# TensorE's products of zeros at the layer changes and in the first attention heads left out

## The chip, the cores and the metric

The kernel runs on one core of one Trainium2 chip. The metric is the device time of one execution in microseconds. Before the change it is 1459.41 us, the median of three runs from 1458.01 to 1461.78.

## What is computed

Two blocks of a network for 256 tokens of width 1024, batch 1, float32. The first block is one layer: four mixers beside each other (latent attention, pooling, a state-space mixer and a gated recurrence), merged by gates, a feed-forward part and a gate with a side input `p`. The second is two layers: a mixer (dilated attention in the first, stick-breaking attention in the second), and a mixture of experts with 16 experts, each followed by a layer norm.

```python
x = x + merged @ w_out[l]
h2 = rmsnorm(x, g_mlp[l])
x = x + jnp.square(jax.nn.relu(h2 @ w_ff1[l])) @ w_ff2[l]
...
for layer in range(DEPTH_2):
    ...
        mixed = mixer_dilated(x, dil_w_in[occ], dil_w_out[occ], rel_table)
    ...
        mixed = mixer_stick_breaking(x, sb_w_in[occ], sb_w_out[occ])
    ...
    x = layer_norm(DEEPNORM_ALPHA * x + mixed, ln1_g[layer], ln1_b[layer])
    ffn = moe_ffn(x, router_w, router_b, exp_w_gate[layer], exp_w_up[layer], exp_w_down[layer])
    x = layer_norm(DEEPNORM_ALPHA * x + ffn, ln2_g[layer], ln2_b[layer])
```

## The kernel before

Each engine has its own instruction list, and the lists meet at semaphores. The weights stream once: SyncE's queue loads them in halves into a ring of six places (`w_ring`), ScalarE writes the high part of each as fp16 into `w_hi` (L1356), VectorE the low part into the ring's place (L1729), and TensorE makes three products for each tile: high by high, high by low, low by high. The dense products are those of `gemm_tok` (L687), `split_T` (L967, L969), the feed-forward output (L992), the products of `p` (L1016), and those of the experts (L1145, L1194). When TensorE is through with a half, it signals `w_used`, and the place is loaded anew.

Between two parts of the network the 256 tokens, in two tiles of 128, are normalized: VectorE adds the result from PSUM and makes sums (L2115, L2304), GpSimd takes the reciprocal root (L591), VectorE scales into `x_norm` (L1723, L1776). `act_transposes` (L657 to L670) then turns each tile on TensorE, 8 transposes of 128x128 for each (L668), and ScalarE and VectorE copy them as high and low parts (L1356, L1734) or as float32 (L1355, L1722). The next dense products wait for that. The document numbers these places by the argument of `act_transposes`: change 1 is ahead of `w_out`, 2 ahead of the feed-forward part, 3 ahead of the gate with `p`, 4 ahead of the dilated attention's projections, 5 and 7 ahead of the experts, 6 ahead of the stick-breaking projections. In changes 5 and 7 the router's 32 products (L1139, float32, 16 columns each) come first.

`idle_turns(n, bank)` (L652 to L655) issues n products of a zero tile, 128x128 by 128x512 in bfloat16, into a PSUM bank that nobody reads before it is written again. They are issued behind the last real product and ahead of the wait for the first normalized tile (`before` of `act_transposes`: 12), behind the transposes (4, in change 6 eight), ahead of the products of `p` (L1008: 12) and in change 1 (L951 and L954: 10 and 4).

The attentions run in stages over 8 pairs of heads, with an order written out by `staged`. In the dilated attention (L1113 to L1121) each step has the late scores (`dil_late`, L1048), turns of older probabilities (L1075), the early scores (`dil_early`, L1061) and the products with the values (L1106, L1109); VectorE adds a bias from GpSimd (L623) and takes maxima (L2231, L2235), ScalarE the exponentials (L1584). Zeros stand in its first two steps: 8 ahead of the late scores and 6 behind them. In the stick-breaking attention (L1323 to L1327) a step has `sb_pv` (L1319), `sb_scores` (L1295, L1296) and `sb_r` (L1305, L1307); VectorE clips (L2522, L2527) and ScalarE takes exponentials and logarithms (L1703, L1711, L1693), with a table load for each switch between them. Zeros stand in its steps 1 to 3: 8, 12 and 8.

Of the kernel before, what the change touches and what calls it, by code (L numbers as in the profile page):

```python
# [27 lines left out]
P = 128  # L28
# [144 lines left out]
def build(nc, a, out):  # L173

    ctx = ExitStack()
    with ctx:
        sems = {}

        def sig(name):
            if name not in sems:  # L180
                sems[name] = ctx.enter_context(nc.semaphore(name))
            return sems[name]

        def sb(name, shape, dt=F32):
            return ctx.enter_context(nc.sbuf_tensor(name, shape, dt))
# [17 lines left out]
        ps = ctx.enter_context(nc.psum_tensor("ps", [P, 8, 512], F32))  # L203
# [82 lines left out]
        zero16 = sb("zero16", [P, 512], BF16)  # L286
# [102 lines left out]
        def staged(i, *stages):  # L389

            for stage, behind in stages:
                if 0 <= i - behind < H2 // 2:
                    stage(i - behind)
# [244 lines left out]
        def _(pe):  # L638
# [10 lines left out]
                        ins = pe.transpose(ps[:, first_bank + k // 2, o:o + P], src[:, t, k * P:(k + 1) * P], ident)  # L649
                    ins.then_inc(sig(sem_name), 1)  # L650

            def idle_turns(n, bank):  # L652

                for _ in range(n):
                    pe.matmul(ps[:, bank, :], zero16[:, 0:P], zero16[:, :], start=True, stop=True)  # L655

            def act_transposes(i, before=None):  # L657

                if i:
                    pe.wait_ge(sig("xp_act"), 4 * i)  # L660
                    pe.wait_ge(sig("xp_dve"), 4 * i)
                if before is not None:
                    idle_turns(12, before)
                for t in range(T):
                    pe.wait_ge(sig(f"xn{t}_ready"), i + 1)
                    for k in range(KD):
                        o = (k % 2) * 256 + t * P
                        ins = pe.transpose(ps[:, 4 + k // 2, o:o + P], x_norm[:, t, k * P:(k + 1) * P], ident)  # L668
                        if t == T - 1:
                            ins.then_inc(sig("xp_pe"), 1)  # L670
# [69 lines left out]
            for c in range(KM):  # L740
                o = (c % 2) * S
                pe.matmul(ps[:, 4 + c // 2, o:o + S], up[:, 0, c * P:(c + 1) * P], band[:, c, 0:S],
                          start=True, stop=False, skip_group_check=True)
                ins = pe.matmul(ps[:, 4 + c // 2, o + P:o + S], up[:, 1, c * P:(c + 1) * P], band[:, c, S:384],
                                start=False, stop=True, skip_group_check=True)
# [6 lines left out]
            for b, k0, kn in ((0, 0, 2), (1, 2, 1)):  # L752
                w_h, w_l = weights(10 + b)
                for t in range(T):
                    hi, lo = slice(t * P, (t + 1) * P), slice(S + t * P, S + (t + 1) * P)
                    for h in range(2):
                        c = slice(h * 384, (h + 1) * 384)
                        for k in range(kn):
                            for i, (u, v) in enumerate(((hi, w_h), (hi, w_l), (lo, w_h))):
                                ins = pe.matmul(ps[:, 4 + 2 * t + h, 0:384], cT[:, k0 + k, u], v[:, k, c],  # L760
                                                start=(k0 + k + i == 0), stop=(k0 + k == 2 and i == 2),
# [14 lines left out]
            for b in range(2):  # L776
                w_h, w_l = weights(14 + b)
                for t in range(T):
                    hi, lo = slice(t * P, (t + 1) * P), slice(S + t * P, S + (t + 1) * P)
                    for h in range(2):  # L780
                        c = slice(h * 512, (h + 1) * 512)
                        for i, (u, v) in enumerate(((hi, w_h), (hi, w_l), (lo, w_h))):
                            ins = pe.matmul(ps[:, 4 + 2 * t + h, :], cT[:, 3 + b, u], v[:, 0, c],
                                            start=(b + i == 0), stop=(b == 1 and i == 2), skip_group_check=True)
# [163 lines left out]
                branch(i, yT, 1, 1)  # L948

            pe.wait_ge(sig("branch"), 3)  # L950
            idle_turns(10, 0)  # L951
            pe.wait_ge(sig("branch"), 4)
            act_transposes(1)
            idle_turns(4, 0)  # L954
            gemm_tok(22, 0, 512, 1)
            gemm_tok(23, 2, 512, None, True)

# [12 lines left out]
                                            stop=(kk == KD - 1), skip_group_check=True)  # L970
                    ins.then_inc(sig("w_used"), 1)

            act_transposes(2, 4)
            idle_turns(4, 0)
            for i in range(8):
                if i >= 2:
                    pe.wait_ge(sig("ff1_out"), i - 1)
# [4 lines left out]
            for i in range(8):  # L982
                pe.wait_ge(sig("hid_lo"), i + 1)
                for b in range(2):
                    w_h, w_l = weights(2 * (FF0 + 8 + i) + b)
                    for t in range(T):
                        for k in range(2):
                            kk = KM * i + 2 * b + k
                            c = slice(t * P, (t + 1) * P)
                            for u, v in ((hid_hi, w_h), (hid_hi, w_l), (hid_lo, w_h)):  # L990
                                for h in range(2):
                                    ins = pe.matmul(ps[:, 2 * t + h, :], u[:, kk, c], v[:, k, h * 512:(h + 1) * 512],  # L992
                                                    start=(kk == 0 and u is hid_hi and v is w_h),
                                                    stop=(kk == 31 and u is hid_lo), skip_group_check=True)
# [10 lines left out]

            pe.wait_ge(sig("pT"), 1)
            pe.wait_ge(sig("rel_row"), 1)
            idle_turns(12, 4)  # L1008
            pe.wait_ge(sig("x_res"), 2)
            for b in range(2):  # L1010
                w_h, w_l = weights(80 + b)
                for t in range(T):
                    hi, lo = slice(t * P, (t + 1) * P), slice(S + t * P, S + (t + 1) * P)
                    for i, (u, v) in enumerate(((hi, w_h), (hi, w_l), (lo, w_h))):
                        for h in range(2):
                            ins = pe.matmul(ps[:, 2 * t + h, :], pT[:, b, u], v[:, 0, h * 512:(h + 1) * 512],  # L1016
                                            start=(b + i == 0), stop=(b == 1 and i == 2), skip_group_check=True)
# [5 lines left out]
            def qkv(n0, g, base, aT, ready):  # L1023

                for s in range(6):
                    pe.wait_ge(sig("qkv_out"), base + 1 + s + g * 6)
                    if s < 4:
                        split_T(n0 + s, aT, (s % 2) * 4, ready, g * 12)
                    else:
                        gemm_tok(n0 + s, (s % 2) * 4, 512, None, False, aT, g * 12)  # L1030

            pe.wait_ge(sig("ple_gate"), 3)
            act_transposes(4)
            idle_turns(4, 0)
            with pe.Fori(0, 3) as g:
                qkv(DIL0, g, 0, act16, lambda b: act_ready(4, b))
            pe.wait_ge(sig("qkv_out"), 20)
# [73 lines left out]
                ins.then_inc(sig("dil_pv"), 1)  # L1111

            for i in range(KD + 2):  # L1113
                if i < 2:
                    idle_turns(8, 7)
                staged(i, (dil_late, 0))
                if i < 2:
                    idle_turns(6, 7)
                staged(i, (lambda m: dil_turn(m, 5), 2), (lambda m: dil_turn(m, 0), 1), (dil_early, 0),
                       (lambda m: dil_turn(m, 1), 1), (lambda m: dil_turn(m, 2), 1), (dil_spread, 1), (dil_pv, 2),  # L1120
                       (lambda m: dil_turn(m, 3), 1), (lambda m: dil_turn(m, 4), 1))  # L1121
# [7 lines left out]

            def experts(layer, n0, turn):  # L1130

                act_transposes(turn, 4)
                idle_turns(4, 0)
                pe.wait_ge(sig("xp_act"), 4 * turn + 4)
                pe.wait_ge(sig("xp_dve"), 4 * turn + 4)
                pe.wait_ge(sig("ld_router"), 16)
                for t in range(T):
                    for k in range(KD):
                        ins = pe.matmul(ps[:, 0, t * NE:(t + 1) * NE], actT[:, k, t * P:(t + 1) * P], router_w[:, k, :],  # L1139
                                        start=(k == 0), stop=(k == KD - 1))  # L1140
# [140 lines left out]

            experts(0, MOE0, 5)

            act_transposes(6, 4)
            idle_turns(8, 0)
            qkv(SBI0, 0, 18, sbq16, lambda b: pe.wait_ge(sig("aT_lo"), 3 + b))
            pe.wait_ge(sig("qkv_out"), 26)

# [33 lines left out]

            sb_scores(0)  # L1323
            for i in range(H2 // 2 + 6):
                if 1 <= i < 4:
                    idle_turns((8, 12, 8)[i - 1], 7)
                staged(i, (sb_pv, 6), (sb_scores, -1), (sb_r, 3))  # L1327

            def sb_o_ready(_, b):
# [1252 lines left out]
```

## Time and profile before

| what | value |
|---|---|
| median of three runs | 1459.41 us |
| the profiled execution | 1456.31 us, span 1454.5 us |
| TensorE matmul busy | 1375.5 us, 95% of the span, 7578 products |
| TensorE weight loads busy | 754.6 us, 52% |
| VectorE busy | 923.7 us, 64% |
| ScalarE busy | 698.4 us, 48% |
| GpSimd busy | 93.2 us, 6% |
| mean granted TensorE clock | 0.984 |

The span is the time from the first to the last instruction of the profiled execution; 1.8 us of its time lie around it. Matmuls are pipelined and overlap in the record, so a busy TensorE is not one at its peak. The granted clock is 1.0 at 2.4 GHz and 0.5 at 1.2 GHz. An engine's idle time costs something only where it is on the chain that ends last.

### The profile page before, as it was taken

How to read it: one execution, taken by the hardware profiler on the slowest of the kernel's cores; microseconds unless marked ns; L12 is line 12 of the kernel's file. 1: busy time of each engine (PE TensorE's matmuls, PEld its weight loads, DVE VectorE, ACT ScalarE, POOL GpSimd, SP SyncE). 2: the span in 40 equal slices, each digit the busy share in tenths (PEclk: the TensorE clock that was granted, in tenths of full speed). 3: DMA queues.
4: the chain of work that ended last, by engine and by line, in shares of the span. 5: the costliest groups of instructions: out<-in, count | busy, mean ns of one | idle time of the engine just before them, and what ended most of it. 6: DMA issues, size and time to landing. Idle time of an engine off the chain costs nothing.

```text
span 1454.5 us, 18623 instructions
## 1 busy us (share of the span) xinstructions
PE 1375.5 (95%) x7578; PEld 754.6 (52%) x7578; DVE 923.7 (64%) x1106; ACT 698.4 (48%) x682; POOL 93.2 (6%) x56
## 2 busy tenths in 40 slices
PE   6999997799999889999999999999989999999996
PEld 4685554345644436555567545444445545454442
DVE  6586755767864575555576575575666757665574
ACT  5476765235543344444456335454534653454451
POOL 0000000000000021000042021000004000300000
PEclk9999999899999989999999999999999999999999
DMA  9475433455656635666610446676837222666682
GB/s 316 131 242 174 145 127 126 147 173 172 218 189 207 233 125 180 204 201 202 202 52 2 145 146 211 223 260 212 309 117 231 86 87 96 214 212 222 212 269 78
DMA packets 152649, 258.03 MB, mean 177 GB/s; under 512 B 8881, under 2 KB 81532, under 8 KB 152572
## 3 DMA queue, kind: packets, MB, share of 16 engines
q1 hardware_dynamic: 152572, 256.96, 53.7%
q8 instruction: 54, 0.88, 0.2%
q14 instruction: 23, 0.19, 0.0%
HBM read 255.87 MB, written 1.07 MB: 177 GB/s over the span
## 4 chain that ended last, share of the span: by engine, by line
PE 86%; DVE 6%; ACT 3%; issue 3%; DVEq 1%; DMA 1%; POOL 1%; SPq 0%; POOLq 0%; ACTq 0%
PE ps L1145 17%; PE ps L687 17%; PE ps L967 11%; PE ps L1194 11%; PE ps L969 6%; PE ps L992 5%; PE ps L702 3%; PE ps L921 2%; DVE w_ring L1729 1%; PE ps L655 1%; ACT w_hi L1356 1%; PE ps L1075 1%; PE ps L1223 1%; PE ps L1182 1%; PE ps L1106 1%
## 5 line engine op out<-in xcount | busy, mean ns | idle before, releaser
L1729 DVE SCALAR_TENSOR_TENSOR w_ring<-w_ring,w_hi 128x2048 f16<-128x2048 f32 (+2 forms) x206 | 465.0, 2270 | 203.2 <-ACT w_hi L1356 202.0
L1356 ACT ACTIVATE w_hi<-w_ring 128x2048 f16<-128x2048 f32 (+2 forms) x206 | 381.9, 1865 | 250.1 <-PE ps L687 69.8
L687 PE MATMUL ps<-w_hi,actT 128*128 128x512 f16 (+2 forms) x832 | 247.5, 377 | 5.7 <-DVE actT L1734 5.7
L967 PE MATMUL ps<-actT,w_hi 128*128 128x512 f16 x640 | 208.6, 379 | 1.5 <-issue 1.2
L969 PE MATMUL ps<-actT,w_ring 128*128 128x256 f16 x640 | 174.6, 273 | 0.0
L687 PE MATMUL ps<-w_ring,actT 128*128 128x512 f16 (+2 forms) x416 | 156.9, 377 | 0.0
L1145 PE MATMUL ps<-w_ring,arena 128*128 128x512 f16 x384 | 146.3, 381 | 0.0
L1356 ACT ACTIVATE arena<-ps 128x512 f16<-128x512 f32 (+6 forms) x87 | 60.6, 709 | 172.2 <-PE ps L969 78.7
L1145 PE MATMUL ps<-w_hi,arena 128*128 128x512 f16 x448 | 138.4, 379 | 0.0
L687 PEld LDWEIGHTS ps<-w_hi,actT 128*128 128x128 f16 x832 | 82.2, 99 | 100.7 <-issue 6.5
L1194 PE MATMUL ps<-w_hi,arena 128*128 128x512 f16 x384 | 102.5, 379 | 2.8 <-DVE arena L2459 2.8
L967 PEld LDWEIGHTS ps<-actT,w_hi 128*128 128x128 f16 x640 | 62.7, 98 | 78.3 <-issue 3.2
L1145 PE MATMUL ps<-arena 128*128 128x512 f16 x320 | 100.3, 383 | 0.0
L1729 DVE SCALAR_TENSOR_TENSOR w_ring<-w_ring,arena 128x2048 f16<-128x2048 f32 x32 | 72.6, 2290 | 23.6 <-ACT arena L1356 23.6
L1194 PE MATMUL ps<-w_ring,arena 128*128 128x512 f16 x256 | 76.1, 379 | 0.0
L1145 PEld LDWEIGHTS ps<-w_hi,arena 128*128 128x128 f16 x448 | 44.1, 99 | 50.3
L969 PEld LDWEIGHTS ps<-actT,w_ring 128*128 128x128 f16 x640 | 62.7, 98 | 7.6
L992 PE MATMUL ps<-w_hi,arena 128*128 128x512 f16 x256 | 66.0, 379 | 0.0
L687 PEld LDWEIGHTS ps<-w_ring,actT 128*128 128x128 f16 x416 | 41.0, 99 | 45.8 <-issue 1.1
L591 POOL TENSOR_TENSOR stats<-stats 128x1 f32<-128x1 f32 x14 | 9.6, 688 | 842.1 <-DVE stats L2326 509.5
L1194 PEld LDWEIGHTS ps<-w_hi,arena 128*128 128x128 f16 x384 | 37.4, 98 | 48.3 <-DVE arena L2459 3.6
L1637 ACT ACTIVATE arena<-ps 128x512 f32<-128x512 f32 x16 | 9.6, 597 | 109.6 <-PE ps L1145 109.6
(411 smaller groups left out, 1840.4 us busy)
## 6 DMA issues: line engine op xcount, KB each, us to landing
w_ring<-in_dil_w_in SPq DMA_DIRECT2D x36, 1024.0 KB, 5.1
w_ring<-in_w_ff SPq DMA_DIRECT2D x32, 1024.0 KB, 5.2
w_ring<-in_exp_w_gate SPq DMA_DIRECT2D x64, 512.0 KB, 4.0
w_ring<-in_exp_w_up SPq DMA_DIRECT2D x64, 512.0 KB, 5.1
w_ring<-in_exp_w_down SPq DMA_DIRECT2D x32, 1024.0 KB, 5.0
w_ring<-in_w_in SPq DMA_DIRECT2D x24, 1024.0 KB, 5.2
w_ring<-in_sb_w_in SPq DMA_DIRECT2D x12, 1024.0 KB, 5.6
w_ring<-in_w_branch SPq DMA_DIRECT2D x8, 1024.0 KB, 5.0
```

Of the source, the lines that this page charges most:

```text
L655: pe.matmul(ps[:, bank, :], zero16[:, 0:P], zero16[:, :], start=True, stop=True)
L687: ins = pe.matmul(ps[:, bank + t, 0:cols], aT[:, kk, u], v[:, k, :], start=(kk + i == 0), stop=(kk == KD - 1 and i == 2), skip_group_check ...
L702: ins = pe.matmul(ps[:, bank + c // 2, o:o + S], v[:, k, cols], act16[:, kk, u:u + S], start=(kk + i + c % 2 == 0), stop=(kk == KD - 1 and ...
L921: ins = pe.matmul(ps[:, 4 * (i % 2) + 2 * t + h, :], yT[:, kk, u], v[:, k, h * 512:(h + 1) * 512], start=(kk + j == 0), stop=(kk == KM - 1 ...
L967: pe.matmul(ps[:, bank + c, :], w_h[:, k, cols], aT[:, kk, :], start=(kk == 0), stop=False, skip_group_check=True)
L969: ins = pe.matmul(ps[:, bank + c, 0:S], w_l[:, k, cols], aT[:, kk, 0:S], start=False, stop=(kk == KD - 1), skip_group_check=True)
L992: ins = pe.matmul(ps[:, 2 * t + h, :], u[:, kk, c], v[:, k, h * 512:(h + 1) * 512], start=(kk == 0 and u is hid_hi and v is w_h), stop=(kk ...
L1075: ins = pe.transpose(ps[:, 5 + i % 2, k * P:(k + 1) * P], e[:, k * P:(k + 1) * P], ident)
L1145: ins = pe.matmul(ps[:, bank, :], u[:, kk, c], v[:, k, :], start=(kk + m == 0), stop=(kk == KD - 1 and m == 2))
L1194: ins = pe.matmul(ps[:, 2 * t + h, :], u[:, b, c], v[:, f, h * 512:(h + 1) * 512], start=False, stop=(last and f == 1 and u is hT_lo), ski ...
L1356: return act.activation(dst, src, ACT.Copy, scale=scale)
L1729: dve.scalar_tensor_tensor(out=lo16(h)[:, 0:kn * c], in0=w_ring[:, h % RING, 0:kn * c], scalar=W_POW, in1=hi16(h)[:, 0:kn * c], op0=ALU.mu ...
```

## The change

It takes out `idle_turns`, all its calls and the argument `before` of `act_transposes`: 154 products in one execution. All waits stay, in their order. The four products of zeros that open the accumulation of the experts (L1276) stay too.

```diff
-            def idle_turns(n, bank):
-
-                for _ in range(n):
-                    pe.matmul(ps[:, bank, :], zero16[:, 0:P], zero16[:, :], start=True, stop=True)
-
-            def act_transposes(i, before=None):
+            def act_transposes(i):
 
                 if i:
                     pe.wait_ge(sig("xp_act"), 4 * i)
                     pe.wait_ge(sig("xp_dve"), 4 * i)
-                if before is not None:
-                    idle_turns(12, before)
                 for t in range(T):
...
             pe.wait_ge(sig("branch"), 3)
-            idle_turns(10, 0)
             pe.wait_ge(sig("branch"), 4)
             act_transposes(1)
-            idle_turns(4, 0)
             gemm_tok(22, 0, 512, 1)
...
-            act_transposes(2, 4)
-            idle_turns(4, 0)
+            act_transposes(2)
...
             pe.wait_ge(sig("rel_row"), 1)
-            idle_turns(12, 4)
             pe.wait_ge(sig("x_res"), 2)
...
             act_transposes(4)
-            idle_turns(4, 0)
...
             for i in range(KD + 2):
-                if i < 2:
-                    idle_turns(8, 7)
                 staged(i, (dil_late, 0))
-                if i < 2:
-                    idle_turns(6, 7)
...
-                act_transposes(turn, 4)
-                idle_turns(4, 0)
+                act_transposes(turn)
...
-            act_transposes(6, 4)
-            idle_turns(8, 0)
+            act_transposes(6)
...
             for i in range(H2 // 2 + 6):
-                if 1 <= i < 4:
-                    idle_turns((8, 12, 8)[i - 1], 7)
                 staged(i, (sb_pv, 6), (sb_scores, -1), (sb_r, 3))
```

## Rows read from the trace of the kernel before

**Rows 1.** Page: granted clock in 40 slices, in tenths; ending chain by engine.

```profile
PEclk9999999899999989999999999999999999999999
...
PE 86%; DVE 6%; ACT 3%; issue 3%; DVEq 1%; DMA 1%; POOL 1%; SPq 0%; POOLq 0%; ACTq 0%
```

**Rows 2.** Products of zeros, line L655: ns shortest/median/longest, first and last start.

```profile
L655 PE MATMUL ps<-zero x154: 378/379/634, 292.6 to 1206.5; 128*128 128x512 bf16 x154
```

**Rows 3.** Windows of busy us per engine; PEclk is the granted clock.

```profile
core 0: us, PE busy (x) PEld busy (x) DVE busy (x) ACT busy (x) POOL busy (x), PEclk, DMA share, GB/s
225.70:229.00 3.30, 3.30 (x13) 1.92 (x13) 3.13 (x8) 3.27 (x6) 0.00 (x0) 0.50 0.00 0
508.90:512.30 3.40, 3.40 (x9) 1.19 (x10) 2.64 (x5) 3.40 (x4) 0.00 (x0) 0.50 0.31 114
536.30:543.00 6.70, 4.36 (x15) 2.51 (x16) 5.89 (x13) 3.95 (x9) 5.10 (x3) 0.50 0.00 1
821.20:833.20 12.00, 10.43 (x72) 7.41 (x70) 8.89 (x13) 4.95 (x8) 0.81 (x2) 1.00 0.27 88
1068.80:1072.10 3.30, 3.30 (x12) 1.86 (x11) 1.90 (x4) 2.82 (x5) 0.00 (x0) 0.50 0.00 0
1212.10:1215.50 3.40, 3.40 (x10) 1.19 (x9) 3.40 (x3) 0.79 (x1) 0.00 (x0) 0.50 0.00 0
```

**Rows 4.** Timeline, change 4: start, us, engine, line, tiles, count, idle before.

```profile
538.33 1.97 PE L668 MATMUL ps<-mats,x_norm 128*128 128x128 f32 x8 [2.90 <-DVE x_norm L1723]
540.09 1.91 PE L655 MATMUL ps<-zero 128*128 128x512 bf16 x4
542.31 0.60 PE L967 MATMUL ps<-actT,w_hi 128*128 128x512 f16 x1 [0.31 <-DVE actT L1734]
```

**Rows 5.** Line L829, weight loads: 60 to 220 us; then 225 to 229.

```profile
L829 PEld LDWEIGHTS ps<-arena x10: 192/192/192, 145.8 to 207.1; 128*128 128x128 f32 x10
...
L829 PEld LDWEIGHTS ps<-arena x2: 333/333/333, 226.2 to 226.5; 128*128 128x128 f32 x2
```

**Rows 6.** Timeline, layer change 1: the zeros.

```profile
292.61 2.32 PE L655 MATMUL ps<-zero 128*128 128x512 bf16 x10
```

**Rows 7.** Timeline, layer change 2.

```profile
320.23 2.75 PE L655 MATMUL ps<-zero 128*128 128x512 bf16 x12
...
327.78 0.38 PE L967 MATMUL ps<-actT,w_hi 128*128 128x512 f16 x1 [1.21 <-issue]
```

**Rows 8.** Timeline, before the products of p.

```profile
495.19 2.75 PE L655 MATMUL ps<-zero 128*128 128x512 bf16 x12
...
499.82 0.60 PE L1016 MATMUL ps<-w_hi,arena 128*128 128x512 f16 x2 [1.88 <-DVE x_tok L2161]
```

**Rows 9.** Timeline, last transposes of layer change 5 and the router.

```profile
825.71 1.09 PE L668 MATMUL ps<-mats,x_norm 128*128 128x128 f32 x8 [0.83 <-DVE x_norm L1776]
...
828.41 3.72 PE L1139 MATMUL ps<-router_w,actT 128*128 128x16 f32 x32 [0.74 <-ACT actT L1355]
```

**Rows 10.** Timeline, layer change 6.

```profile
1068.35 1.68 PE L668 MATMUL ps<-mats,x_norm 128*128 128x128 f32 x8 [3.38 <-DVE x_norm L1776]
...
1069.83 3.02 PE L655 MATMUL ps<-zero 128*128 128x512 bf16 x8
```

**Rows 11.** Timeline, first two head pairs of the dilated attention.

```profile
731.10 1.90 PE L655 MATMUL ps<-zero 128*128 128x512 bf16 x8 [1.32 <-DVE arena L1723]
...
734.64 0.96 DVE L2231 CUSTOM_DVE_ANT_0 x_norm<-ps,ln_gb 128x768 f32<-128x768 f32 x1 [3.60 <-PE ps L1048]
...
738.53 1.57 PE L1048 MATMUL ps<-arena 64*128 64x256 f32 x12
...
740.14 0.96 DVE L2231 CUSTOM_DVE_ANT_1 arena<-ps,w_ring 128x768 f32<-128x768 f32 x1 [1.83 <-PE ps L1048]
```

**Rows 12.** Timeline, stick-breaking heads: a VectorE wait, a ScalarE wait.

```profile
1145.40 0.96 DVE L2522 SCALAR_TENSOR_TENSOR arena<-ps,mats 128x768 f32<-128x768 f32 x1 [1.96 <-PE ps L1296]
...
1154.90 0.84 ACT L1703 ACTIVATE arena<-arena 128x768 f32<-128x768 f32 x1 [1.06 <-DVE arena L2527]
```

## The prediction

> **What bounds the kernel now.** I read the page first. TensorE is the bound: the chain that ended last is 86% TensorE, and nothing else has more than 6% of it [rows 1]. What it gets done per microsecond hangs on its granted clock, which the same page shows at 9 tenths or more in all 40 slices [rows 1]. So two questions decide this change: which of the removed products stand on TensorE's chain, where each returns its own time, and what the clock does when TensorE has nothing to do in their place.
>
> The second view is the line of the zeros (L655): 154 products, 379 ns each in the record [rows 2]. They overlap: twelve take 2.75 us together and ten 2.32 [rows 6, 7], so one more of them costs (2.75 - 2.32) / 2 = 0.215 us at 2.4 GHz. Where the clock is at half they take longer: four 1.91 us, eight 3.02 [rows 4, 10].
>
> The third view is the windows. It shows what a lost clock looks like: in 508.9 to 512.3, 536.3 to 543.0, 1068.8 to 1072.1 and 1212.1 to 1215.5 the granted clock is 0.50, that is 1.2 GHz [rows 3]. TensorE was quiet ahead of such stretches: 2.90 us idle, eight transposes, then zeros still at the slow pace [rows 4]; or 3.38 us idle ahead of the transposes of change 6 [rows 10]. It rose again only behind dense products: 3.4 us of them from 508.9 and from 1212.1, and 540.09 to 543.0, 2.9 us, in change 4 [rows 3, 4]. Half the pace over 2.9 to 3.4 us of dense work costs 1.45 to 1.7 us. I take 1.6 us as the price of one resumption at 1.2 GHz. With zeros in the gaps the same sequence of work kept 1.00 all the way from 821.2 to 833.2, though not at the same place one layer later, where it was 0.50 from 1212.1 [rows 3]. So the zeros help, they do not guarantee it.
>
> **The change part by part.** It removes 154 products and adds no wait; every wait of TensorE stays in its place, and the other queues keep their orders. Weights that SP's queue loads are released by the last real product ahead of each group of zeros, which is not moved.
>
> *Layer changes, direct time.* In changes 1, 2, 4, 5, 6 and 7 and ahead of the products of p, TensorE waits again behind the zeros, for VectorE or for the evacuation of the transposes: idle 1.21 us behind those of change 2, 1.88 us ahead of L1016, 0.74 us ahead of the router [rows 7 to 9]. The cover that hides the zeros is the normalization on VectorE and GpSimd, and removing them returns nothing there. In change 4 the wait behind four slow zeros is still 0.31 us [rows 4]. Direct gain: 0 (bound 0.3 us in all).
>
> *Layer changes, clock.* Here is the cost. Site by site, each time with 1.6 us for a slow resumption of dense products:
> - Change 1 (10 + 4 zeros, [rows 6]): the pauses are short. Three chances in ten of a slow resumption: 0.5 us (0 to 1.7).
> - Change 2 (12 + 4): without zeros the pause from 320.23 to 327.78 holds 16 transposes only [rows 7], much like that of change 4, which was slow. 1.6 us, and 0.2 for transposes that feed ScalarE at half the pace: 1.8 (0.1 to 2.4).
> - Ahead of L1016 (12): 499.82 - 495.19 = 4.6 us without any work [rows 8], then 24 dense products. 1.6 us (0 to 2.4).
> - Change 4 (4): slow already, but zeros carry 1.91 us of the slow stretch and real products only 543.0 - 542.31 = 0.7 us of it, 0.35 lost [rows 4]. Without them the products pay: 1.6 - 0.35 = 1.3 (0 to 1.7).
> - Changes 5 and 7, the two expert layers (12 + 4 each): the first dense work behind the pause is preceded by the router, 32 small products in 3.72 us, on the chain, since the wait ahead of it ends with ScalarE's copies and the experts' products follow at once [rows 9]. They move 16 columns each and are bound by their fp32 weight loads. Those loads take 192 ns at full clock and 333 at half [rows 5], the second in the stretch from 225.7 that has a clock of 0.50 [rows 3], so the router would take 3.72 * 333/192 = 6.5 us, or up to twice 3.72: 2.7 to 3.7 more. I take 2.5, because the transposes at half pace may lift the clock in some runs. A slow resumption follows, 1.6, less what is paid now (0 in one layer, 1.7 in the other [rows 3]: 0.85 on average). Together 2.5 + 1.6 - 0.85 = 3.25 a layer, 6.5 for both (0.6 to 9.9).
> - Change 6 (12 + 8): now the eight zeros absorb the slow stretch and the products begin behind it [rows 3, 10]. Without them 1.6 (0 to 2.4).
>
> Sum: 0.5 + 1.8 + 1.6 + 1.3 + 6.5 + 1.6 = 13.3 us lost.
>
> On the router a page speaks otherwise. The Trainium skill (TensorE: Matmul & The Clock Gate, LDWEIGHTS) gives a weight load as its columns over 1.2 GHz, the same whatever the array's level. By it the router would stay at 3.72 us and the total below would be 5.0 us smaller. The loads of L829 contradict it with 192 against 333 ns, and the measurement decides.
>
> *First heads of the dilated attention (8 + 6 + 8 + 6).* Here zeros stand on the chain. VectorE waits 3.60 us for the first scores, of which the eight zeros in front are 1.73 us, and 1.83 us again for the second, L1048 at 738.53 [rows 11]. Without zeros the first scores come 1.73 us earlier, and the second can start when VectorE's second maximum is done, which I put at 734.64 plus two times 0.96 and some 0.5 us of small steps, 737.1 (an estimate), 1.4 us before they do now. Together the heads run ahead by 1.73 + 1.4 = 3.1 us, never more than 1.73 + 1.83 = 3.6: I take 3.2. The next limit is VectorE and the bias on GpSimd, then TensorE itself. Against it: little work is left in these 10 us, so one slow stretch is likely (8 in 10, 1.6 us: 1.3; bounds 0 and 3.4). Net 1.9 gained (3.6 gained to 0.5 lost).
>
> *First heads of the stick-breaking attention (8 + 12 + 8).* VectorE waits 1.96 us for scores behind zeros, but ScalarE bounds these heads; the only wait it has for VectorE there is 1.06 us, at 1154.90 [rows 12]. At most that comes back: 1.0. A slow stretch may cost 0.6 (0 to 1.7). Net 0.4 gained (1.1 gained to 1.2 lost).
>
> **Total.** 13.3 - 1.9 - 0.4 = +11.0 us. The profiled execution took 1456.31 us (span 1454.5 and 1.8 around it) and becomes 1467.3. It lies 3.1 us under the median of 1459.41, so as a median I expect 1470.4. A measurement here can tell 0.3%, 4.4 us, from no change.
>
> **The rivals.**
> - *The clock comes back early.* Transposes and products at half pace count as enough work, so that the clock rises before the router and most resumptions are fast. For it: eight slow transposes take 1.97 us and fill the pause better than at 2.4 GHz. Against it: eight of them in change 4 did not lift it [rows 3, 4]. Then the router costs nothing and the sites pay about two thirds: 2/3 * (13.3 - 5.0) - 1.9 - 0.4 = +3.2, 1462.6 (1460 to 1465).
> - *Every pause costs in full.* All sites at their upper ends, router at twice 3.72: 1.7 + 2.4 + 2.4 + 1.7 + 9.9 + 2.4 = 20.5 us, less 1.9 and 0.4: +18, 1477.6.
> - *Faster.* Zeros on the chain in the heads return 3.2 + 1.0 us and the clock does not fall any more often than now: -4.2 at most, 1455.7 with the smallest clock costs. The place is L1048 in the first two steps; it decides if the clock costs at the layer changes stay under 4 us. For it: 28 zeros on the chain. Against it: the clock is lost in this trace even with zeros [rows 3].
> - *Nothing comes out of it*, since weight preparation on VectorE bounds behind each change and hides a slow TensorE: 1459.4. Against it: the 86% of the chain.
>
> **How the numbers follow.** Forecast (+7 to +16) 0.60, early return 0.22, every pause 0.09, faster 0.05, nothing 0.04. The range 1461.0 to 1478.5 leaves out the last two, the lowest of the second and a little above. Over 0.3% slower (above 1463.8): 0.60 + 0.09 + a third of 0.22 = 0.76. Faster by over 0.3%: under half of 0.05, 0.02. Within: 0.22.
>
> **What would show it.** Right: more stretches at 0.50 in the windows, at 324 to 331, 498 to 505, 824 to 838 and 1203 to 1217; L1139's 32 products in 6 to 7.5 us; L1048's second group some 3 us earlier relative to its first wait. Wrong: a clock of 1.00 over the routers, or idle time of TensorE behind weights, where slow products would have been hidden.

## The result and the profile after

| | before | after |
|---|---|---|
| median | 1460.6 us (4 runs, 1458.01 to 1462.02) | 1475.47 us (4 runs, 1471.05 to 1478.35) |
| profiled execution | 1456.31 us, span 1454.5 | 1471.05 us, span 1469.2 |
| mean granted clock | 0.984 | 0.965 |

The four runs of the kernel before are the three of the section above and one more. The changed kernel is slower: the ratio is 1.0101, with a 95% interval of 1.0068 to 1.0135, and the medians lie 14.9 us apart. A second timing, at the end of the experiments, puts them 10.9 us apart. The page of the changed kernel, whose lines answer to [rows 1] (the span; busy us of each engine; the granted clock in 40 slices; the chain by engine):

```profile
span 1469.2 us, 18315 instructions
...
PE 1360.5 (93%) x7424; PEld 750.9 (51%) x7424; DVE 923.7 (63%) x1106; ACT 698.4 (48%) x682; POOL 93.3 (6%) x56
...
PEclk9999999889999989999999899999989998999998
...
PE 85%; DVE 5%; ACT 4%; issue 3%; DVEq 1%; DMA 1%; POOL 1%; SPq 0%; ACTq 0%; POOLq 0%
```

TensorE has 154 products fewer and 15 us less to do, and the span is 14.7 us longer. VectorE, ScalarE and GpSimd have the same busy times as before to 0.1 us. Seven slices stand at 8 tenths of the clock, where the page of before has two [rows 1].

The windows say where. Each line is a stretch, its length, busy us and instructions of each engine, PEclk, DMA share and GB/s; it answers to [rows 3]:

```profile
core 0: us, PE busy (x) PEld busy (x) DVE busy (x) ACT busy (x) POOL busy (x), PEclk, DMA share, GB/s
297.20:303.80 6.60, 5.58 (x17) 2.32 (x16) 5.03 (x9) 4.04 (x9) 0.00 (x0) 0.50 0.18 71
327.90:334.50 6.60, 4.66 (x15) 2.20 (x16) 6.42 (x10) 4.14 (x8) 0.00 (x0) 0.50 0.01 2
502.00:508.60 6.60, 4.18 (x10) 1.46 (x11) 5.46 (x7) 3.26 (x1) 0.79 (x2) 0.50 0.34 133
539.50:553.00 13.50, 9.42 (x34) 5.57 (x34) 11.38 (x17) 4.83 (x9) 9.94 (x4) 0.50 0.12 46
829.60:843.10 13.50, 12.01 (x48) 9.58 (x49) 10.52 (x18) 5.41 (x8) 0.00 (x0) 0.50 0.02 7
1075.40:1088.90 13.50, 7.43 (x25) 4.06 (x26) 9.92 (x12) 7.54 (x8) 0.55 (x1) 0.50 0.00 1
1218.80:1228.80 10.00, 9.20 (x38) 7.71 (x39) 8.46 (x11) 3.99 (x6) 0.00 (x0) 0.50 0.01 2
730.00:760.00 30.00, 25.61 (x226) 17.90 (x225) 21.23 (x49) 16.62 (x36) 12.60 (x7) 1.00 0.26 88
```

A stretch at 0.50 is called a fall from here on. At every change of layer but change 3, and at the products of `p`, there is now one of 6.6 to 13.5 us, where before the longest in this part was 6.7 us [rows 3]. In the order of time these lines are changes 1, 2, the products of `p`, changes 4, 5, 6 and 7. Only the last line, the start of the dilated heads, is at 1.00.

Apart from the zeros both traces hold the same sequence of products, so each can be followed from one to the other. How much later the first product of each part starts than in the kernel before (the last column is what the part adds by itself):

| place | before, us | after, us | later by | its own share |
|---|---|---|---|---|
| change 1 to first feed-forward product | 327.78 | 329.84 | 2.06 | +2.1 |
| change 2 to first product of L992 | 410.98 | 415.37 | 4.39 | +2.3 |
| products of `p` and change 3, to the transposes of change 4 | 534.36 | 539.36 | 5.01 | +0.6 |
| change 4, to the first projection by `gemm_tok` | 584.26 | 591.74 | 7.48 | +2.5 |
| dilated heads, to the first product of their output | 800.52 | 804.70 | 4.18 | -3.3 |
| change 5: router | 828.41 | 833.06 | 4.65 | +0.5 |
| change 5: first expert product | 831.97 | 839.88 | 7.90 | +3.3 |
| to the transposes of change 6 | 1063.88 | 1073.50 | 9.62 | +1.7 |
| change 6, to `gemm_tok` of the projections | 1115.22 | 1127.74 | 12.52 | +2.9 |
| stick-breaking heads, to their output | 1179.76 | 1191.70 | 11.95 | -0.6 |
| change 7: first expert product | 1211.20 | 1226.42 | 15.21 | +3.3 |
| end | 1454.5 | 1469.2 | 14.7 | -0.5 |

The shares sum to 14.7 us: 18.6 lost at the changes of layer, 3.9 gained in the heads. In change 7 the last line gives 0.5 back, since the kernel before had a stretch at 0.50 there too [rows 3].

The router is the dearest single group. Its line in the changed kernel (ns shortest, median, longest), and the timeline of change 5, which answers to [rows 9]:

```profile
L1122 PEld LDWEIGHTS ps<-router_w,actT x64: 286/333/333, 833.0 to 1226.1; 128*128 128x128 f32 x64
L1122 PE MATMUL ps<-router_w,actT x64: 364/374/374, 833.1 to 1226.2; 128*128 128x16 f32 x64
```

```profile
829.90 1.97 PE L661 MATMUL ps<-mats,x_norm 128*128 128x128 f32 x8 [2.20 <-DVE x_norm L1756]
...
833.06 6.98 PE L1122 MATMUL ps<-router_w,actT 128*128 128x16 f32 x32 [1.19 <-ACT actT L1335]
...
839.88 0.59 PE L1128 MATMUL ps<-arena 128*128 128x512 f16 x1
```

The 32 instructions take 6.98 us, against 3.72 [rows 9], and their weight loads 333 ns, as those of L829 do at half clock [rows 5]. The eight transposes ahead of them, at half pace too (1.97 us, against 1.09 [rows 9]), did not lift the clock before the router.

Change 4, which answers to [rows 4]:

```profile
543.34 1.97 PE L661 MATMUL ps<-mats,x_norm 128*128 128x128 f32 x8 [2.06 <-DVE x_norm L1703]
...
547.32 0.60 PE L958 MATMUL ps<-actT,w_hi 128*128 128x512 f16 x1 [2.02 <-DVE actT L1714]
```

The first projection product starts at 547.32, and the stretch at 0.50 lasts to 553.0: 5.7 us of dense products at half pace, 2.8 us lost at this place alone. In the kernel before the zeros had begun 2.2 us ahead of the first product, and it saw the full clock 0.7 us after its start [rows 4].

The first two steps of the dilated heads, which answer to [rows 11]:

```profile
738.58 1.57 PE L1036 MATMUL ps<-arena 64*128 64x256 f32 x12 [1.32 <-DVE arena L1703]
...
740.29 0.96 DVE L2211 CUSTOM_DVE_ANT_0 x_norm<-ps,ln_gb 128x768 f32<-128x768 f32 x1 [1.76 <-PE ps L1036]
...
742.73 1.57 PE L1036 MATMUL ps<-arena 64*128 64x256 f32 x12 [1.91 <-DVE mx L2222]
...
744.34 0.96 DVE L2211 CUSTOM_DVE_ANT_1 arena<-ps,w_ring 128x768 f32<-128x768 f32 x1 [0.37 <-PE ps L1036]
```

VectorE waits 1.76 us for the first scores instead of 3.60, and 0.37 us for the second instead of 1.83. The second scores start 4.15 us behind the first (738.58 to 742.73) and now wait for VectorE's maximum.

### The profile page after: what moved, and what is told of

It reads as the page before. It is cut to its first block, busy times and chain, and to the rows that moved or that the text cites. A ratio compares the mean times of both kernels' runs of the same rounds, so it can differ in the third digit from the quotient of the medians.

```text
span 1469.2 us, 18315 instructions
## 1 busy us (share of the span) xinstructions
PE 1360.5 (93%) x7424; PEld 750.9 (51%) x7424; DVE 923.7 (63%) x1106; ACT 698.4 (48%) x682; POOL 93.3 (6%) x56
## 4 chain that ended last, share of the span: by engine, by line
PE 85%; DVE 5%; ACT 4%; issue 3%; DVEq 1%; DMA 1%; POOL 1%; SPq 0%; ACTq 0%; POOLq 0%
PE ps L1128 17%; PE ps L680 17%; PE ps L958 12%; PE ps L1177 11%; PE ps L960 6%; PE ps L982 5%; PE ps L695 2%; PE ps L914 2%; DVE w_ring L1709 1%; ACT w_hi L1336 1%; PE ps L1063 1%; PE ps L1122 1%; PE ps L1206 1%; PE ps L1165 1%; PE ps L1094 1%
## 5 line engine op out<-in xcount | busy, mean ns | idle before, releaser
L958 PE MATMUL ps<-actT,w_hi 128*128 128x512 f16 x640 | 213.2, 385 | 4.1 <-issue 2.1
L591 POOL TENSOR_TENSOR stats<-stats 128x1 f32<-128x1 f32 x14 | 9.7, 690 | 846.6 <-DVE stats L2306 508.9
```

The lines of the kernel that those rows point to most:

```text
L958: pe.matmul(ps[:, bank + c, :], w_h[:, k, cols], aT[:, kk, :], start=(kk == 0), stop=False, skip_group_check=True)
```

## The experiments

Two theories stood against each other. The clock theory: at the changes of layer the zeros keep TensorE's clock up and cost nothing, in the heads they are on the chain and cost their own time. Against it stood that the zeros matter by their presence in TensorE's queue, that the heads need them as well, and that the router has no price of its own.

**Zeros out of the heads only.**

```diff
             for i in range(KD + 2):
-                if i < 2:
-                    idle_turns(8, 7)
                 staged(i, (dil_late, 0))
-                if i < 2:
-                    idle_turns(6, 7)
...
             for i in range(H2 // 2 + 6):
-                if 1 <= i < 4:
-                    idle_turns((8, 12, 8)[i - 1], 7)
```

> Only the zeros in the first heads of the two attentions are left out (28 + 28); those of the layer changes stay. Clock theory: the zeros of the heads are on TensorE's chain and buy nothing there. The trace of the changed kernel puts their own time at 3.3 us in the dilated attention (the stretch from L1048's first scores to the next dense products) and 0.6 us in the stick-breaking one, and shows no stretch at 0.50 in the heads. So 1460.6 - 3.9 = 1456.7 us (1454 to 1459). Rival, the heads need their zeros for the clock as well: a fall in each, 1.6 to 2.9 us twice, takes the gain back, 1459 to 1462.

Measured: 1457.48 us beside 1460.07 for the kernel before, ratio 0.9986 (0.9971 to 1.0). The timeline of the first two steps:

```profile
731.51 1.57 PE L1048 MATMUL ps<-arena 64*128 64x256 f32 x12 [1.32 <-DVE arena L1717]
...
735.66 1.57 PE L1048 MATMUL ps<-arena 64*128 64x256 f32 x12 [1.92 <-DVE mx L2236]
...
737.27 0.96 DVE L2225 CUSTOM_DVE_ANT_1 arena<-ps,w_ring 128x768 f32<-128x768 f32 x1 [0.37 <-PE ps L1048]
```

The second scores start 4.15 us behind the first and VectorE's second wait is 0.37 us, as in the changed kernel. The dilated heads are 3.3 us shorter and the stick-breaking ones 0.6 us: the direct prices are right. The gain in the median, 2.6 us, is smaller than 3.9, and its interval touches 1, so the time alone does not show a gain here.

**The same kernel again, for a second trace.**

> The kernel without zeros in the heads once more, for a second trace and for times beside the two others on one chip. Its first trace has no fall in the dilated heads and one in the stick-breaking heads. If falls there depend on the moment at which the heads come, this trace may show another pattern, and the time is 1457.5 within 1.5 us; if the place alone decided, the same pattern.

Measured: 1456.94 us beside 1462.46, ratio 0.996 (0.9938 to 0.9983). In its trace the dilated heads are 3.3 us shorter again, but the stick-breaking heads have a fall at 1146.6 and another at 1170.5, and take 1.0 us longer than in the kernel before, not 0.6 less. In the first trace there was one at 1144.2 and none near 1170; the kernel before has none near 1145, and one at 1167.7. So the pattern of the falls is not the same in two executions of one kernel. Behind change 3, where the code is that of the kernel before, this trace has no fall, and gets 1.7 us back there.

**Zeros out of the changes of layer only.**

```diff
-            act_transposes(2, 4)
-            idle_turns(4, 0)
+            act_transposes(2)
...
-                act_transposes(turn, 4)
-                idle_turns(4, 0)
+                act_transposes(turn)
```

(and in the same way in changes 1, 4 and 6 and ahead of the products of `p`).

> Only the zeros of the layer changes and ahead of the products of p are left out (98); those of the heads stay. Clock theory: the whole loss stands at the layer changes and the heads' zeros cost 3.9 us more, so 1475.5 + 3.9 = 1479.4 us (1476 to 1482), the slowest of the four. Rival, the heads' zeros pay for themselves: 1475.5 or a little less.

Measured: 1477.94 us, ratio 1.0126 (1.0106 to 1.0146), 17.9 us above the kernel before. The whole loss is here, and with the heads' zeros kept the median lies 2.5 us above that of the changed kernel; 3.9 were forecast, which the intervals don't exclude. In its trace the dilated heads take the same time as before to 0.01 us.

**Zeros in the two expert layers only.** As the changed kernel, with `act_transposes(turn, 4)` and `idle_turns(4, 0)` kept in `experts`.

> Zeros only in changes 5 and 7 (32 of 154), all others left out. Clock theory with the router as the dearest place: the changed kernel loses 5.4 us in change 5 and 2.7 us in change 7 against the kernel before (by its trace), so 1475.5 - 8.1 = 1467.4 us (1465 to 1470), and the router's 32 products are back near 3.7 us in at least one layer. Rival, each pause costs the same and the router nothing of its own: 18.6 us over seven places, two of them back, 1475.5 - 5.3 = 1470.2 us.

Measured: 1467.61 us, ratio 1.0047 (1.003 to 1.0064). The router and the first expert product of its trace:

```profile
838.02 3.72 PE L1130 MATMUL ps<-router_w,actT 128*128 128x16 f32 x32 [0.74 <-ACT actT L1343]
...
841.59 0.38 PE L1136 MATMUL ps<-arena 128*128 128x512 f16 x1
```

32 of the 154 products bring back 7.9 us of the changed kernel's median, near the 8.1 that the shares of the table give (5.4 + 2.7). The intervals of the two ratios also hold the 5.3 of equal prices, so the time does not decide; the trace does. The router is at 3.72 us again in both layers, 6.5 us less for the two than in the changed kernel, so it does have a price of its own. In this trace the resumptions at changes 2, 4 and 6, which have no zeros here either, cost 2.1, 1.7 and 1.6 us.

**Thin products in the zeros' place, twice.**

```diff
                 for _ in range(n):
-                    pe.matmul(ps[:, bank, :], zero16[:, 0:P], zero16[:, :], start=True, stop=True)
+                    for _ in range(2):
+                        pe.matmul(ps[:, bank, 0:16], zero32[:, 0:P], zero32[:, 0:16], start=True, stop=True)
```

> Each product of zeros of the kernel before is replaced by two of float32 with 16 columns, which take the same time (2 x 0.116 us as the router's, against 0.215) and load as many weights, but do a sixteenth of the columns. Clock theory: this is no work, the clock falls as without zeros, and in the heads these products stand on the chain, some of them at half pace: 1475.5 + 3.9 = 1479.4 us or more, up to 1486. Rival, it is enough that TensorE has instructions (its queue, its order, its weight loads), whatever they do: as before, 1460.6 us.

Measured: 1528.9 us, ratio 1.0467 (1.0445 to 1.049), outside both expectations. The line of the thin products explains it:

```profile
L658 PE MATMUL ps<-zero x616: 179/263/396, 296.4 to 1279.0; 128*128 128x16 f32 x154
```

616 records for 308 products: a float32 product is carried out in two. Each product of zeros had become 0.44 us of thin ones and not 0.23, so they outgrew the waits. The 0.116 us that the expectation took from the router are those of a record too: the router's 32 products are 16 in the code (eight for each tile), in two records each. The design was at fault, and the run decides nothing between the theories; the next one repairs it.

**Thin products, one for one** (the diff above without the inner loop).

> As the run before with float32 products of 16 columns in the place of the zeros, but one for one: the trace of that run shows that a float32 product is recorded twice (616 records for 308), so there each product of zeros had been replaced by 0.44 us of thin ones, not 0.23. Here it is 154 of them, 0.22 us each at full clock, against 0.215 for those of 512 columns: the time that TensorE is occupied is the same. Clock theory: the clock falls as without zeros, and the thin products, on the chain in the heads and at half pace 0.43 us each, cost their own time on top: 1479.4 plus 3 to 20 us, 1490 in the middle. Rival, any occupation of TensorE of the same length keeps the clock: 1460.1 us.

Measured: 1487.87 us, ratio 1.0186 (1.0155 to 1.0216). Windows of the dilated heads and the timeline through them:

```profile
741.00:744.20 3.20, 3.20 (x16) 2.37 (x15) 0.00 (x0) 0.00 (x0) 0.00 (x0) 0.50 0.62 210
744.30:747.80 3.50, 3.50 (x36) 3.25 (x34) 3.02 (x9) 1.89 (x2) 0.00 (x0) 0.99 0.01 2
748.00:751.20 3.20, 3.20 (x16) 2.81 (x18) 0.23 (x3) 2.34 (x8) 2.82 (x2) 0.50 0.00 0
747.80:758.00 10.20, 10.20 (x51) 8.61 (x51) 2.69 (x10) 3.94 (x11) 3.57 (x2) 0.50 0.00 0
```

```profile
746.71 2.68 PE L657 MATMUL ps<-zero 128*128 128x16 f32 x16
...
749.33 2.93 PE L1050 MATMUL ps<-arena 64*128 64x256 f32 x12
...
752.19 2.74 PE L657 MATMUL ps<-zero 128*128 128x16 f32 x12
```

From 744.3 to 747.8 TensorE is busy without a pause at the full clock, with thin products and scores. Then the clock falls, and it stays at 0.50 for 10.2 us, in which TensorE is busy without a pause too. So it isn't the presence of instructions that keeps the clock: with the same count, the same places and the same time at full clock the falls at the changes of layer are there as without them, and the heads, which have none at these places with zeros, have them too. The thin products differ from the zeros in their columns and in their type, float32 for bfloat16; which of the two counts was not tested. At half pace six thin products (twelve records) take 2.74 us on the chain, where six of zeros took some 0.215 us each, and the heads grow by 6.7 and 5.1 us.

**Only the zeros ahead of the products of `p` left out** (`idle_turns(12, 4)` at L1008).

> Of the kernel before, only the 12 zeros ahead of the products of p are left out. The prediction priced them at 1.6 us. The trace of the changed kernel gives another figure: from the products of p to the next transposes it loses 2.1 to 2.3 us, but 1.7 of it come back at change 3, because the fall that the kernel before has there (0.50 from 508.9) is gone. So by the first 1461.7 us, by the second 1460.7, too close in time alone; the place of L687 behind change 3 tells them apart: 1.6 us later than in the kernel before, or 0.6. Rival, the wait there is long enough without them and nothing changes: 0.

Measured: 1464.93 us beside 1461.89, ratio 1.0026 (1.0013 to 1.0038). The windows, and the first products of `p` and the transposes behind them:

```profile
498.70:505.30 6.60, 5.31 (x13) 1.96 (x14) 5.34 (x6) 2.10 (x1) 0.55 (x1) 0.50 0.16 63
512.30:515.50 3.20, 3.20 (x10) 1.09 (x8) 2.44 (x4) 3.20 (x2) 0.00 (x0) 0.50 0.11 40
```

```profile
499.99 1.01 PE L1015 MATMUL ps<-w_hi,arena 128*128 128x512 f16 x2 [4.70 <-DVE x_tok L2160]
...
507.83 1.91 PE L668 MATMUL ps<-mats,x_norm 128*128 128x128 f32 x16
```

Neither figure is right. The 24 products of `p` run from 499.99 to 507.83, 7.8 us, against 5.2 before, so the price of one resumption is 2.65 us. The fall behind change 3 is there as well (512.3), so nothing comes back. In this trace the routers run partly at half pace too (1.8 and 1.9 us lost), with all their zeros in place. Whether that follows from the twelve products can't be told from one trace; the kernel with only its heads' zeros moved, below, has it as well.

**The waits of the changes filled further, no zeros in the heads.**

```diff
-            def act_transposes(i, before=None):
+            def act_transposes(i, before=None, first=12, between=0):
...
                 for t in range(T):
+                    if t:
+                        idle_turns(between, 0)
...
-            idle_turns(12, 4)
+            idle_turns(20, 4)
...
-            act_transposes(4)
-            idle_turns(4, 0)
+            act_transposes(4, 4, 12, 12)
+            idle_turns(8, 0)
```

> The kernel without zeros in the heads, and with more of them at the layer changes, so that what is left of idle time there is filled: 20 ahead of the products of p, 3 to 14 between the transposes of the first tile and the second (12 in change 4, 14 in change 6, 3 in the others that had 12 in front), 7 to 16 behind them, and 12 in front in change 4. Clock theory: the falls of changes 4 and 6 go, worth some 1.5 to 2.5 us together, and those ahead of L1145 stay, since they come from the router: 1457.5 - 2 = 1455.5 us (1452 to 1458). Rival, the added products no longer fit into the waits and stand on the chain: 1459 us or more.

Measured: 1456.66 us, ratio 0.997 (0.995 to 0.9989). Its windows over change 4 and over the starts of both attentions:

```profile
536.30:543.00 6.70, 5.53 (x34) 3.23 (x34) 6.68 (x11) 4.82 (x9) 6.52 (x2) 1.00 0.00 0
733.90:740.70 6.80, 6.16 (x36) 4.16 (x33) 4.15 (x16) 4.75 (x13) 3.59 (x2) 0.50 0.00 0
1140.10:1150.30 10.20, 8.62 (x33) 5.83 (x30) 7.23 (x10) 10.03 (x12) 0.00 (x0) 0.50 0.01 2
```

Change 4 is at 1.00 all through and change 6 has no fall either; those ahead of the experts' first products stay (829.4 and 1211.7), as expected. The same trace has falls of 6.8 and 10.2 us in the heads, which have no zeros now. From the first scores to the output the dilated heads take 0.8 us longer than with zeros and 2.2 us longer than without zeros and without a fall: of the 3.3 us that the zeros cost in these heads, 1.5 lie behind the first scores, and this fall costs 2.2. The kernel without zeros in the heads, from which this one differs by the fuller waits alone, had a ratio of 0.9986; the intervals of the two overlap, so what the fuller waits are worth is not shown.

**Zeros in the heads only where TensorE waits anyway**, on top of the kernel just shown.

```diff
+            idle_turns(6, 7)
             pe.wait_ge(sig("qkv_out"), 20)
...
                 staged(i, (dil_late, 0))
+                if i == 1:
+                    idle_turns(4, 7)
...
+                if i == 0:
+                    idle_turns(7, 7)
...
+                if i == 1:
+                    idle_turns(4, 7)
+                staged(i, (sb_pv, 6), (sb_scores, -1))
+                if i == 3:
+                    idle_turns(8, 7)
+                staged(i, (sb_r, 3))
```

> The kernel with the gaps of the layer changes filled, and with zeros in the heads again, but only where TensorE waits anyway: 6 between the last projection and the wait for its evacuation, 7 and 4 behind the scores of the first two steps of the dilated attention, 4 and 8 between stages of the stick-breaking one. Its forerunner lost 2.2 us to a fall in the dilated heads and up to 2 us to one in the stick-breaking heads. If zeros in waits keep the clock there at no price of their own: 1456.7 - 3 = 1454 us (1451 to 1456). Rival, they are still on the chain, or too few to keep the clock: 1456.7 or more.

Measured: 1452.42 us beside 1462.46, ratio 0.994 (0.9919 to 0.996). This version beats both kernels. Its clock line, and windows over change 4, the start of the dilated heads, change 5 and the stick-breaking heads:

```profile
PEclk9999998899999999999999999999999999999998
```

```profile
536.30:546.00 9.70, 8.63 (x47) 4.57 (x45) 7.96 (x16) 4.79 (x10) 4.88 (x3) 1.00 0.34 111
726.00:746.00 20.00, 19.38 (x130) 11.27 (x132) 13.12 (x29) 10.01 (x19) 6.23 (x4) 1.00 0.39 133
829.00:843.00 14.00, 13.95 (x80) 8.10 (x81) 11.43 (x31) 3.03 (x4) 0.00 (x0) 1.00 0.04 9
1137.00:1160.00 23.00, 19.61 (x125) 12.81 (x124) 18.74 (x25) 19.44 (x22) 0.00 (x0) 1.00 0.14 46
```

All four are at 1.00, and the dilated heads are still 3.3 us shorter than in the kernel before. What is left at 0.50 lies ahead of change 1, behind change 3, at 1164.9 and in the last 8 us.

**The heads' zeros moved into the waits, the rest as before.**

> The kernel before with only the heads' zeros moved into the waits, as in the run before this one; its layer changes are untouched. Against the kernel without zeros in the heads (1457.5 us beside 1460.1 for the kernel before) this one tells what the clock in the heads is worth: if the falls in the heads are frequent, 1 to 2 us less, 1456; if they were rare, the same 1457.5. Rival, the moved zeros are on the chain: 1459 to 1461.

Measured: 1454.91 us beside 1462.46, ratio 0.9946 (0.9926 to 0.9967). It is 2.0 us under the kernel without zeros in the heads that was timed beside it (1456.94), which is within their intervals; that this much is the clock in the heads is likely, not shown. Nor can it be told from the kernel before this one (1452.42, ratio 0.994): what both share is the place of the heads' zeros, and that alone gives a gain clear of the noise. In its trace neither attention has a fall at its start, and the dilated heads are 3.3 us shorter. Both routers run partly at half pace (1.6 and 1.2 us lost), with all their zeros in place.

**The changed kernel again.**

> The changed kernel once more, for a second trace and times on this chip. Clock theory: the router's 32 products take near 6.8 us in both expert layers again, the first dense products behind changes 2, 4, 5, 6 and 7 begin at half pace, and the ratio to the kernel before is 1.010 (1.008 to 1.013). Rival, the falls were chance: the ratio of this look differs by more than 0.4%.

Measured: 1473.34 us beside 1462.46, 10.9 us more, ratio 1.0093 (1.0068 to 1.0118). Its trace gives the same shares as the first to 0.1 us in changes 4, 5, 6 and 7 and in both heads. Change 2 costs 1.9 us, `p` with change 3 0.2, and change 1 nothing, where the first had 2.1. That trace is 3.7 us later already ahead of change 1, in a part that the change doesn't touch.

## Why the prediction was right, and where its sizes were off

The forecast was +11.0 us, 1470.4 as a median; the medians give +14.9 and 1475.47, inside the range, and +10.9 in the second timing. The direction and the mechanism held. The size is in part luck: in the first trace the changes cost 18.6 us where 13.3 were forecast, and the heads gave 3.9 where 2.3 were, so two misses partly cancel. By its losses at the changes that trace lies nearer to the rival in which every pause costs in full (20.5). Term by term, with the shares of the two traces of the changed kernel:

| term | predicted | first trace | second trace |
|---|---|---|---|
| change 1 | +0.5 | +2.1 | 0.0 |
| change 2 | +1.8 | +2.3 | +1.9 |
| ahead of the products of `p` (with change 3) | +1.6 | +0.6 | +0.2 |
| change 4 | +1.3 | +2.5 | +2.5 |
| change 5 | +3.25 | +5.4 | +5.4 |
| change 6 | +1.6 | +2.9 | +2.9 |
| change 7 | +3.25 | +2.75 | +2.7 |
| dilated heads | -1.9 | -3.3 | -3.3 |
| stick-breaking heads | -0.4 | -0.6 | -0.6 |
| sum | +11.0 | +14.7 | +11.8 |

*What bounds the kernel* held. TensorE's chain took up both the lost clock and the zeros of the heads, and no other engine hid anything. The rival in which nothing comes out of it, and that in which the kernel gets faster, fell with the result; the faster one had its direct price nearly right (4.2 us, measured 3.9) and its condition wrong, since the clock cost 18.6 us and not under 4.

*Direct time at the changes: nothing.* Right. In change 4 TensorE waits 2.02 us behind the last transposes with the zeros gone, and the first projection product starts later by 5.0 us (542.31 [rows 4], 547.32), as the transposes ahead of it do.

*The price of one resumption, 1.6 us.* This term was too small: changes 2, 4 and 6 together are 3.0 us short in the first trace. I read it from the kernel before, whose stretches at 0.50 with dense products in them lasted 2.9 to 3.4 us [rows 3, 4]. In change 4 zeros stood ahead of the products there and took up most of the slow time. Without them the slow stretch held 5.7 us of dense work in change 4 and 5.6 in change 6 (first product at 1083.44, full clock from 1089.0). The prices came out at 1.9 to 2.9 in changes 2, 4 and 6, and at 2.65 with `p` alone taken out. They are not fixed, though: with zeros in the expert layers alone the fall of change 4 lasted 10.2 us instead of 13.5 and cost 1.7, close to the forecast. What decides the length of a fall stays open.

*The clock before.* The prediction read the page as 9 tenths or more in all 40 slices; two of them stand at 8 [rows 1]. Its sum doesn't use that reading.

*The router, 2.5 us a layer.* Also too small: 3.26 in both layers and both traces. The discount, for transposes at half pace that might lift the clock, was not due; the estimate from the weight loads, 2.7 to 3.7, holds it. The rival of an early return rested on the same hope. The Trainium skill (TensorE: Matmul & The Clock Gate, LDWEIGHTS) gives a load's time as its columns over 1.2 GHz and names no level of the clock. That does not hold for these float32 loads: 192 ns at full clock became 333 at half, and the router 6.98 us instead of 3.72.

*The products of `p`.* As the changed kernel shows it, too large: 0.6 and 0.2 instead of 1.6. The step that failed was to count this place alone. The kernel before pays a fall behind change 3 already, from 508.9 [rows 3]; the changed one pays 2.1 us (1.7 in the second trace) at the products of `p` and gets 1.7 back behind change 3, where its trace has no fall. Taken out by itself, the same edit cost 2.65 us at its place and nothing came back, because there the second fall stayed. That return is in part chance: the kernel without zeros in the heads, in its second trace, and the one with them moved have no fall behind change 3 either, with this part as before.

*Heads.* The direct gain of 3.2 us was right (3.3), and the wait that follows is VectorE's maximum, as put. The 1.3 and 0.6 us for new falls there did not show in either trace of the changed kernel: its one fall in the stick-breaking heads stands behind nearly the same work as one of the kernel before, which the prediction did not show.

```profile
1167.70:1171.10 3.40, 3.40 (x13) 2.00 (x13) 2.73 (x3) 3.37 (x4) 0.00 (x0) 0.50 0.00 0
1177.70:1181.10 3.40, 3.40 (x13) 2.09 (x14) 2.62 (x2) 2.76 (x5) 0.00 (x0) 0.50 0.00 0
```

The first line is the kernel before, the second the changed one. New falls do exist in other traces. Of the six without zeros in the heads two have one at the start of the dilated heads and four at the start of the stick-breaking ones; of the five with products of 512 columns there, on the chain or in waits, none has. That speaks for the heads' zeros keeping the clock there, without proving it, and the 8 chances in 10 for the dilated heads look too many.

What stays open is the part of chance. The runs of one kernel differ by up to 9.6 us (the kernel before, 1453.77 to 1463.38), and two traces of the changed kernel by 3.7 us at a place that the change does not touch. The shares of the second trace sum to 11.8, close to the forecast; the medians are 14.9 and 10.9 apart.

## What to carry to other kernels

Work that keeps TensorE's clock up belongs into its waits and nowhere else: look in the timeline at which engine ended each wait, put it behind the last real product and ahead of the wait, and where a dependency is already fulfilled leave it out. Here moving the heads' zeros into waits was worth 0.5% to 0.6%, and leaving all zeros out cost 1.0%. Price a lost clock by what comes next, dense products and small ones bound by their weight loads alike, and read that price from a place that has no such filling ahead of it. Take a second trace before a single fall is put down to a change.

## What the runs showed of the hardware

- A TensorE that is busy without a pause can lose its clock and stay without it: 3.5 us of 3.5 busy at PEclk 0.99 with float32 products of 16 columns and scores, then 10.2 of 10.2 us busy at 0.50.
- Float32 weight loads slow down with the clock, 192 to 333 ns, and with them products that are bound by the load: 3.72 to 6.98 us for 32.
- A float32 product leaves two matmul records: 616 for 308, and 32 for the 16 of the router. A float32 transpose leaves one (x16 for two tiles of eight).
- Where falls lie differs between executions of one kernel (1144.2, or 1146.6 and 1170.5). Routers with all their zeros in place ran at full clock in some traces and lost 1.2 to 1.9 us in two others.
